# A gate's half steps beside the last causal head, and maxima read bank by bank

## The reference: what is computed

```python
# first block: causal softmax attention with a forget gate (8 heads of 64), beside a retention branch
s = einsum('bhqd,bhkd->bhqk', q_blk, kh) * scale + c_blk[..., None] - c[:, :, None, :]
s = where(mask, s, -inf);  o_f = einsum('bhqk,bhkd->bhqd', softmax(s), vh)
merged = sigmoid(a_r) * (o_r @ w_ret_o) + sigmoid(a_f) * (o_f @ w_fox_o)      # a_r, a_f: columns of h @ w_in
x = x + merged @ w_out
...
# second block: attention from latents (8 heads of 64 + 32 rotary dimensions), no mask
s = einsum('bqhd,bkhd->bhqk', q_blk, k);  out = einsum('bhqk,bkhd->bqhd', softmax(s), v)
```

## Time and profile before

| what | us |
|---|---|
| median of 3 runs | 3119.72 (3118.37 to 3121.61) |
| the profiled execution | 3124.64 |
| its span, first to last instruction | 3122.9 |
| PE busy | 3003.2, 96% |
| DVE busy | 1279.3, 41% |
| POOL busy | 1142.2, 37% |
| ACT busy | 938.9, 30% |
| mean granted clock of PE | 0.988 |

### The profile page before, as it was taken

How to read it: one execution, slowest core, us unless ns; L and a number is a source line. 1 busy time by engine, 2 the same in 40 slices (tenths; PEclk the granted TensorE clock), 3 DMA queues, 4 the chain that set the end, 5 groups by cost and what they waited for, 6 DMA issues and landing times.

```text
span 3122.9 us, 39113 instructions
## 1 busy us (share of the span) xinstructions
PE 3003.2 (96%) x14522; PEld 2398.3 (77%) x14522; DVE 1279.3 (41%) x1649; ACT 938.9 (30%) x1546; POOL 1142.2 (37%) x893
## 2 busy tenths in 40 slices
PE   7999998999999999999999999999999999999998
PEld 6778776788777888887887766668788888878876
DVE  2573656311331000002435578860466565661133
ACT  3232555300121000001123356651444444430011
POOL 2424110344445444444445710004434343444445
PEclk9999999999999999999999999999999999999999
DMA  3111000211322111112113310012422323241122
GB/s 129 38 55 45 21 28 14 95 47 47 108 68 84 47 47 47 47 47 101 47 47 114 91 34 14 15 38 71 121 62 78 78 75 84 64 162 47 47 104 88
DMA packets 102914, 202.91 MB, mean 65 GB/s; under 512 B 14608, under 2 KB 27664, under 8 KB 102288
## 3 DMA queue, kind: packets, MB, share of 16 engines
q1 hardware_dynamic: 65808, 123.53, 13.8%
q10 hardware_dynamic: 36992, 77.77, 7.5%
HBM read 157.22 MB, written 31.46 MB: 60 GB/s over the span
## 4 chain that ended last, share of the span: by engine, by line
PE 78%; DVE 11%; ACT 4%; issue 2%; POOL 2%; DMA 1%; ACTq 0%; POOLq 0%; SPq 0%; DVEq 0%
PE ps L348 32%; PE ps L364 13%; PE ps L309 11%; PE ps L1869 7%; PE ps L1072 3%; PE ps L1103 1%; PE ps L2073 1%; DMA raw<-in_stream_dram 1%; DVE mla_ptl L1036 1%; ACT ps L1012 1%; POOL wl L3070 1%; DVE mla_nm L1045 1%; PE ps L1088 1%; PE ps L1732 1%; POOL wh L3068 1%
## 5 line engine op out<-in xcount | busy, mean ns | idle before, releaser
L3068 POOL TENSOR_TENSOR wh<-raw,zeros 128x512 fp32r<-128x512 f32 x440 | 487.2, 1107 | 1938.8 <-PE ps L348 616.1
L3070 POOL TENSOR_TENSOR wl<-raw,wh 128x512 fp32r<-128x512 f32 x440 | 641.7, 1459 | 34.5
L348 PE MATMUL ps<-hth,wh 128*128 128x512 f32 x1168 | 462.2, 396 | 0.4 <-issue 0.3
L348 PE MATMUL ps<-hth,wl 128*128 128x512 f32 x1168 | 461.8, 395 | 0.0
L348 PE MATMUL ps<-htl,wh 128*128 128x512 f32 x1168 | 461.8, 395 | 0.0
L364 PE MATMUL ps<-hth,wh 128*128 128x512 f32 x704 | 286.9, 408 | 2.1 <-DVE fox_vl L1285 2.1
L364 PE MATMUL ps<-hth,wl 128*128 128x512 f32 x704 | 281.0, 399 | 0.0
L364 PE MATMUL ps<-htl,wh 128*128 128x512 f32 x704 | 280.8, 399 | 0.0
L348 PEld LDWEIGHTS ps<-hth,wh 128*128 128x128 f32 x1168 | 219.3, 188 | 55.3 <-DVE dil_ot L2763 0.7
L348 PEld LDWEIGHTS ps<-htl,wh 128*128 128x128 f32 x1168 | 219.2, 188 | 53.6
L348 PEld LDWEIGHTS ps<-hth,wl 128*128 128x128 f32 x1168 | 219.2, 188 | 53.5
(11 more groups left out here) (429 smaller groups left out, 5634.3 us busy)
## 6 DMA issues: line engine op xcount, KB each, us to landing
raw<-in_stream_dram SPq DMA_DIRECT2D x440, 256.0 KB, 2.7
dil_stg<-dil_stg ACTq DMA_DIRECT2D x96, 128.0 KB, 2.4
dil_sz<-vd_dram ACTq DMA_DIRECT2D x12, 512.0 KB, 4.2
heads_raw<-heads_dram ACTq DMA_DIRECT2D x8, 512.0 KB, 7.4
norm_x<-in_x_dram ACTq DMA_DIRECT2D x1, 4096.0 KB, 16.0
x_dram<-norm_x ACTq DMA_DIRECT2D x8, 512.0 KB, 3.2
down_x<-x_dram ACTq DMA_DIRECT2D x1, 4096.0 KB, 12.9
x_dram<-down_x ACTq DMA_DIRECT2D x8, 512.0 KB, 3.1
```

Source lines behind the costliest of these rows:

```text
L348: ins = nc.tensor.matmul(ps[:, bank + half, :], w[:, j % 2, c:c + P], a[:, k, HALF * half:HALF * half + HALF], start=first and q == 0, sto ...
L3068: nc.gpsimd.tensor_tensor(wh[:, s, :], raw[:, s, :], zeros[:].to_broadcast([P, HALF]), ALU.add).then_inc(w_hi, 1)
L3070: nc.gpsimd.tensor_tensor(wl[:, s, :], raw[:, s, :], wh[:, s, :], ALU.subtract).then_inc(w_split, 1)
```

## The change

1. `Fox.beside_last`, called in `pe_prep` after `project`: in each of slots 80 to 95 one half step (three matmuls) of gate 0, column 0 of the first merge, into banks 2 and 3. The first waits for x.7. With it the merge's first two weight units are used there.
2. `merge1.pe` starts at gate 1 (units from `u["merge1"] + 2`, an empty `first_done`). The sigmoid of gate 0, column 0 reads banks 2 and 3 (`first_bank=2`), and the first head product, which writes these banks, waits for it. The loop's own waits and the order of ACT's work are as before.
3. In `Latents` only (`BANKS_APART`): PE waits for each of the two maxima banks by itself and signals after each matmul; DVE reduces each bank by itself as it comes (two reduces of 512 columns into `two`), and after the fourth block takes the smaller of the negated maxima of both banks (128 x 4), for which the row's matmuls wait.

```diff
+            BANKS_APART = False
...
                     for n, t in self.maxima_at(s):
-                        steps_p.append(f"mx{n}.{t}")
-                        steps_v.append(f"mx{n}.{t}")
+                        steps = [f"ma{n}.{t}"] * self.BANKS_APART + [f"mx{n}.{t}"]
+                        steps_p += steps
+                        steps_v += steps + [f"mm{n}"] * (self.BANKS_APART and t == 3)
...
+            def maxima_apart(self, dve, due):
+                a, v, p = self.a, self.v, self.p
+                for n, t in due:
+                    if n and t == 0:
+                        v.wait(dve, f"mm{n - 1}")
+                    for b, step in enumerate(("ma", "mx")):
+                        p.wait(dve, f"{step}{n}.{t}")
+                        v.did(nc.vector.tensor_reduce(self.two[:, t, b:b + 1], ps[:, self.MAX + b, :], AX, ALU.max, negate=True), f"{step}{n}.{t}")
+                    if t == 3:
+                        v.wait(dve, f"mx{n}.3")
+                        v.did(nc.vector.tensor_tensor(self.nm[:, n, :], self.two[:, :, 0], self.two[:, :, 1], ALU.min), f"mm{n}")
+            def bank_free(self, pe, what, b):
+                k = [use[1] for use in self.max_uses].index(what)
+                line, _, step = self.max_uses[k - 1] if k else (None, None, None)
+                if line == "v":
+                    self.v.wait(pe, ("ma", "mx")[b] + step[2:])
+                elif b == 0:
+                    self.max_free(pe, what)
...
                     due = self.maxima_at(s)
+                    if due and self.BANKS_APART:
+                        self.maxima_apart(dve, due)
+                        due = []
...
-                        if m == 0:
+                        if m == 0 and not self.BANKS_APART:
                             self.max_free(pe, f"mx{n}.{t}")
...
+                            if self.BANKS_APART:
+                                self.bank_free(pe, f"mx{n}.{t}", col // HALF)
+                                if col:
+                                    p.did(ins, f"ma{n}.{t}")
                             ins = nc.tensor.matmul(ps[:, bank, at:at + w], q, k, start=True, stop=True)
...
                         self.max_free(pe, f"r{n}")
+                        if self.BANKS_APART:
+                            v.wait(pe, f"mm{n}")
...
+            FILL = (1,) * 16
...
+            def beside_last(self, pe, s):
+                o = s - (self.n_tiles - 16)
+                if 0 <= o < len(self.FILL):
+                    for n in range(sum(self.FILL[:o]), sum(self.FILL[:o + 1])):
+                        if n == 0:
+                            self.a.wait(pe, f"x.{self.HEADS - 1}")
+                        feature_step(pe, self.fill_unit, n // 2, self.PROJ, self.fill_line, "a0", (n % 2,))
...
                 self.project(pe, s, u0)
+                self.beside_last(pe, s)
...
-                x = ps[:, 4 * br:4 * br + 2, :].rearrange("p a b -> p (a b)")
+                bank = self.first_bank if slot_given is None and (c, br) == (0, 0) else 4 * br
+                x = ps[:, bank:bank + 2, :].rearrange("p a b -> p (a b)")
...
                         v.wait_before(pe, f"m{br}", c)
+                        if br == 0 and self.first_bank:
+                            a.wait(pe, "g0", c)
...
+            fox.fill_unit, fox.fill_line = u["merge1"], merge1.pa
...
-            merge1.pe(pe, u["merge1"], split1.ready)
+            merge1.pe(pe, u["merge1"] + 2, split1.ready, lambda pe: None)
```

More of the change, by code:

```diff
@@ L977, in alloc @@
                 self.Vl = sb(n + "_vl", [P, NT, self.HEADS, 64], F32R, scope)
+                if self.BANKS_APART:
+                    self.two = sb(n + "_two", [P, 4, 2], F32, scope)
                 self.nm = sb(n + "_nm", [P, self.N, 4], F32R, scope)
@@ L1424, in build_two_blocks, with __init__ @@
         class Merge:
-            def __init__(self, name, scope, branches, bias):
-                self.bias = bias
+            def __init__(self, name, scope, branches, bias, first_bank=0):
+                self.bias, self.first_bank = bias, first_bank
                 self.br = branches
@@ L1455, in gate @@
                 self.pa.wait(act, f"a{br}", c)
+                slot_given = slot
                 if slot is None:
@@ L2095, in build_two_blocks @@
             LEAD, RING, PROJ = 2, 3, 3
+            BANKS_APART = True
             MX_AT, ROW_AT = ((-7, -6, -5, -4), (0, 1, 2, 3)), (-3, 4)
@@ L3008, in build_two_blocks @@
         fox = scoped(Fox)
-        merge1 = scoped(lambda s: Merge("merge1", s, (0, 1), None))
+        merge1 = scoped(lambda s: Merge("merge1", s, (0, 1), None, first_bank=2))
         with ExitStack() as s:
```

## The result

The changed kernel takes 3124.54 us, the median of 20 runs (3118.59 to 3128.29), beside 3119.68 (20 runs, 3115.26 to 3122.51) for the kernel before: a ratio of 1.0015, 95% interval 1.0009 to 1.0021. That is 4.9 us slower, between 2.8 and 6.6. I had said 3.3 us more and "no change within 0.2%"; the forecast holds, and the sign is settled by the runs: a small loss.

What follows compares the result with a forecast made beforehand. TensorE, busy 96% of the span, was taken as the bound. Terms -2.5 + 1.5 + 4.0 + 0.3 = +3.3 us took the median from 3119.72 to 3123.0 us, with a range of 3116.5 to 3129.5.

Steps and rivals of the forecast that it cites:

- The moved gate's old place: Start of the first merge: 48 matmuls leave, but the loop still waits for the first sigmoid; -2.5 us, bounds 0 and -3.1.
- the loads slow: First merge: the bound of 0 instead of -2.5 us, if the head loads before the first sigmoid slow by that much.
- The clock after it: First merge: TensorE runs at half clock after standing still there; +1.5 us, from 1.1 to 2.0.
- The new place: Slots 80 to 95 of the causal heads: added half steps are about half hidden; +4.0 us, bounds 2.9 and 11.2.
- the 27 to 28 of my sign: Head 7's first scores to the merge's first matmul: 23.6 us before, 27 to 28 expected.
- The bound of 2.9 from heads 5 and 6: Slots 80 to 95: lower bound in us, from head 5 with sixteen half steps beside head 6 without.
- R1: Rival, last causal slots: half steps uncovered, all 11.2 us on the path, 3130.2 us; chance 0.14.
- The maxima: Latent heads: maxima taken by bank, extra VectorE work against earlier matmuls; +0.3 us, bounds -3.9 and +8.5.
- R2: Rival, latent heads: VectorE becomes the bound, +8.5 instead of +0.3, 3131.2 us; chance 0.12.
- R3: Rival, latent heads: the banks pay at every wait, -3.9 instead of +0.3, 3118.8 us; chance 0.08.
- R4: Rival, latent heads: TensorE never waits for a maximum again, 17.8 us gained, 3104.9 us; chance 0.08.
- the full 11.2 us: First merge: shortening by all of the moved gate's 11.2 us, held impossible while the loop's sigmoid wait stands.

## Why the prediction was right, point by point

- **The moved gate's old place, -2.5.** Right in mechanism: I had named the wait, the releaser and the reason. Measured: the loop starts 21.95 us after the merge's first load, before 23.51, so -1.56. Two things were off. The sigmoid came 20.8 us after the start, not 19.84: more of it in waits for the heads' loads (1.89 before one copy; the longest between copies was 0.80 before). The bound "the loads slow" was in the range. The three profiles with this order on ACT and the half steps have the first sigmoid 20.8 to 20.9 us after the merge's start, the three without half steps 19.7 to 20.3; why the loads land later in the former wasn't tried. The stall was 10.93, not 8.5 (nor 7 to 9, the sign I gave), also because gate 1 alone took 11.0 us (568.18 to 579.20) and not 12.5: PE now enters the merge at full clock.
- **The clock after it, +1.5.** +1.87, inside 1.1 to 2.0. Eleven intervals, not the eight of the earlier trace rows.
- **The new place, +4.0.** +3.73 in this pair of profiles, 3.5 over the nine. Of the 3.73, 0.42 lie before the last head's first scores (I had 0.3) and 3.31 behind them. There the clock gave more back than my 0.9: it is 1.00 for 22 us that had 0.92, which by my estimate is 1.8 us, so the thirteen slots cost some 5.1 and not 4.6. The two errors nearly cancel, which is luck; 5.1 of 9.1 us of matmuls is still about half. The last head's stretch was 26.90, just under the 27 to 28 of my sign. The bound of 2.9 from heads 5 and 6 was near. R1 (11.2, nothing hidden) is out; 30.2 us for the last head, its sign, was seen only with half steps in pairs. That early clock comes back was right (1.00 from 544 to 548).
- **The maxima, +0.3.** +0.08 here; over the profiles with and without, nothing. The parts were fair: a pair of reduces takes 1.28 us against 1.218 for one of 1024 columns, 0.06 where I took 0.08, and the minimum 0.163 where I took 0.21 with its wait. The Trainium skill (VectorE: DVE Perf Modes, "The DRAIN you can't avoid") has the next instruction start only when the pipe is empty, but adds that one that is not held starts earlier. My prediction gave the first half alone. Two reduces of 0.682 in 1.28 overlap by 0.08, which goes with the second half, not against the page. But R2 and R3 were not far-off cases: each is half of what happens. R2's work costs 3.3 to 3.7 when it stands alone, under half of the 8.5 that every instruction on the path would make, and R3's gain, 3.9 by my sum, is what pays for it. That the +0.3 came out near nothing is therefore partly luck: I had priced both parts far smaller. My sign that the waits before the maxima would be fewer was wrong; they are shorter but more, 38 for 26. The period of a latent head is 36.83 us (half of 1863.62 to 1937.28), within the 0.2 that I gave; 37.3 in the kernel that waits for both.
- **R4** and the full 11.2 us did not come, for the reasons given: the second bank's matmul waits instead, and the loop's wait stood.
- **What I missed** is not in the sum but in the reading: I wrote that the gain is impossible "while the loop's wait for the first sigmoid stands" and did not price what one line on ACT would give. Two small sums are off and change nothing: R3 with the slot cost at 2.9, less 1.4, is 3116.3 and not 3116.5, and 0.03 a head over eight heads is 0.2 and not 0.3. My chances put 0.66 on "within 0.2%"; the ratio of 1.0015 lies there, and the range held it.

## What to carry to other kernels

Work moved ahead of a join gains only what its releaser gains: before moving it, follow the first wait behind its old place to the engine that ends it, and ask what stands in front of it on that queue. Here one operation of 1.12 us behind eight copies turned a gain of 9 us into a loss of 4, by the stretches. Filler between an output product and the next scores was best spread as thin as the slots allow: the same sixteen half steps cost 3.5 us one by one and 5 to 6.5 in pairs. Where two effects of an edit may cancel, a kernel that keeps one and drops the other tells more than the edit itself.

## What the runs showed that was not expected

Some 5 us of this kernel's time are decided long before the change. Head 6's first scores come at 509.4 to 510.1 us in five profiles (before, after, and three more) and at 504.5 to 506.9 in the other six, whatever the edit. A part of it is the clock in the first causal head. The changed kernel and the one with the sigmoid first, 300 to 310 us:

```profile
300.00:310.00 10.00, 8.03 (x36) 5.90 (x35) 6.41 (x10) 5.92 (x8) 0.12 (x1) 0.89 0.08 26
```

```profile
300.00:310.00 10.00, 8.03 (x45) 5.95 (x43) 6.57 (x10) 7.02 (x10) 2.65 (x2) 1.00 0.00 0
```

In the five late ones the granted clock is 0.87 to 0.90 there, in the six early ones 1.00, although PE is busy for 8.0 us in all of them. It makes some 1.6 us: from that head's first scores to the second head's the kernel before took 34.90 us (304.75 to 339.65), the one with the new order alone 33.32 (302.54 to 335.86). Another 2.3 us or so are there before that head starts, in five of the six: its first scores come at 302.1 to 302.8, in the others at 304.4 to 304.9. (The sixth is the kernel in which PE waits for both banks, the one with 506.9 at head 6.) Behind the latent heads, where nothing differs either, the eleven profiles take 1020.0 to 1023.9 us to the end. Both may be why medians of 5 to 11 runs of kernels with the same stretches lie 6 us apart; what tips them wasn't tried.

Five copies of 1.06 us that follow each other took 4.84, and three sigmoids of 1.12 took 3.13: back to back, these ACT instructions overlap by 0.1 us each.
